# The first projections of an attention stage, issued in the tail of the stage before it

## The reference

```
h = rmsnorm(x, norm_pre) * (1 + scale) + shift
z = h @ w_in                       # 1024 x 3488, split into 14 parts
o_mla  = mha(q from rmsnorm(m_cq) @ wq_b, k and v from rmsnorm(m_ckv) @ wkv_b)   # 4 heads of 64+32
o_gqa  = gqa(rope(rmsnorm(g_q)), rope(rmsnorm(g_k)), g_v)                        # 4 heads, 2 KV heads
o_diff = softmax(q0 k0) v - lam * softmax(q1 k1) v, rmsnorm over each head       # 4 heads, 2 maps
o_hy   = hyena(hy_in)              # a long convolution of order 2, as DFT matmuls
out = concat(o_g * silu(gate_g) for the four groups) @ w_out
x = x + gate * rmsnorm(out, norm_post)
```

## Time and profile before

| | |
|---|---|
| median of three runs | 2651.21 us |
| the profiled execution, device time | 2656.59 us |
| its span, first to last instruction | 2654.8 us |
| TensorE matmul busy | 2388.5 us, 90% |
| VectorE, ScalarE, GpSimd busy | 1318.4 (50%), 909.7 (34%), 172.8 us (7%) |
| mean granted TensorE clock | 0.961 of 2.4 GHz |
| DMA | 129.11 MB, mean 49 GB/s |

### The profile page before, as it was taken

How to read it: one execution, slowest core, us unless ns; L and a number is a source line. 1 busy time by engine, 2 the same in 40 slices (tenths; PEclk the granted TensorE clock), 3 DMA queues, 4 the chain that set the end, 5 groups by cost and what they waited for, 6 DMA issues and landing times. The chain is left out here.

```text
span 2654.8 us, 36377 instructions
## 1 busy us (share of the span) xinstructions
PE 2388.5 (90%) x14472; PEld 1601.8 (60%) x14472; DVE 1318.4 (50%) x2642; ACT 909.7 (34%) x1826; POOL 172.8 (7%) x183
## 2 busy tenths in 40 slices
PE   3999999898999897989949999998989998889898
PEld 1755775675466766764417657656844666767643
DVE  3352663564556466581133526645644563855711
ACT  1142213452245264371022421134521452644610
POOL 0220001000100000001202200010001000000012
PEclk8999999999999998999959999999999999989999
DMA  6440000100100000012145301001000000001111
GB/s 223 152 162 26 21 31 17 49 2 14 34 32 1 10 3 6 33 34 87 63 156 178 136 26 52 10 7 49 1 14 34 33 1 12 1 6 65 41 64 56
DMA packets 74225, 129.11 MB, mean 49 GB/s; under 512 B 24994, under 2 KB 38178, under 8 KB 72420
## 3 DMA queue, kind: packets, MB, share of 16 engines
q1 hardware_dynamic: 73944, 122.04, 13.4%
q10 hardware_dynamic: 112, 4.72, 0.5%
HBM read 109.54 MB, written 21.92 MB: 50 GB/s over the span
## 5 line engine op out<-in xcount | busy, mean ns | idle before, releaser
L602 PE MATMUL psum<-arena 128*32 128x128 f32 (+8 forms) x9904 | 1727.8, 404 | 114.7 <-DMA arena<-in_hy_decay 47.4
L602 PEld LDWEIGHTS psum<-arena 128*128 128x128 f32 (+3 forms) x9904 | 1044.4, 155 | 735.0 <-issue 515.0
L606 PE MATMUL psum<-ident,arena 128*128 128x128 f32 (+1 forms) x2248 | 354.2, 282 | 92.6 <-ACT arena L1408 39.8
L1581 DVE TENSOR_TENSOR arena<-arena 128x64 f32<-128x64 f32 (+10 forms) x670 | 301.8, 497 | 199.3 <-ACT arena L1537 57.7
L606 PEld LDWEIGHTS psum<-ident,arena 128*128 128x128 f32 (+1 forms) x2248 | 254.5, 141 | 195.5 <-issue 106.0
L602 PE MATMUL psum<-k_parts,q_parts 96*128 96x384 f32 (+2 forms) x1000 | 285.1, 374 | 17.1 <-ACT arena L1332 4.7
L1581 DVE TENSOR_TENSOR arena<-psum,arena 128x512 f32<-128x512 f32 (+2 forms) x116 | 67.1, 580 | 280.4 <-PE psum L602 280.0
L1873 DVE TENSOR_REDUCE st<-psum 128x1 f32<-128x1152 f32 (+1 forms) x144 | 177.9, 1237 | 49.6 <-PE psum L602 49.2
L602 PEld LDWEIGHTS psum<-k_parts,q_parts 96*128 96x128 f32 (+1 forms) x1000 | 171.0, 195 | 34.4 <-issue 18.0
L1951 DVE TENSOR_REDUCE st<-psum 128x1 f32<-128x1152 f32 (+1 forms) x144 | 173.2, 1233 | 36.1 <-PE psum L602 35.9
L1332 ACT ACTIVATE arena<-psum,st 128x1152 f32<-128x1152 f32 (+1 forms) x144 | 162.4, 1128 | 75.6 <-DVE st L1873 72.5
(11 more groups left out here) (132 smaller groups left out, 1324.0 us busy)
## 6 DMA issues: line engine op xcount, KB each, us to landing
arena<-in_ada_w SPq DMA_DIRECT2D x12, 2048.0 KB, 8.8
arena<-in_w_in SPq DMA_DIRECT2D x10, 2048.0 KB, 9.1
arena<-out_xs SPq DMA_DIRECT2D x36, 512.0 KB, 4.8
out_xs<-arena SPq DMA_DIRECT2D x18, 512.0 KB, 2.6
arena<-in_w_out SPq DMA_DIRECT2D x4, 2048.0 KB, 8.5
out_xs<-in_x ACTq DMA_DIRECT2D x1, 4608.0 KB, 17.8
spectrum_kept<-arena SPq DMA_DIRECT2D x2, 2304.0 KB, 8.4
arena<-spectrum_kept SPq DMA_DIRECT2D x2, 2304.0 KB, 8.5
```

Of the source, the lines that this page charges most:

```text
L602: return nc.tensor.matmul(out, lhsT, rhs, start=start, stop=stop)
L606: return nc.tensor.transpose(out, src, ident[0:n, 0:n])
L1581: return nc.vector.tensor_tensor(out, a, b, op)
```

## The change

Four things move.

1. TensorE issues the first projections of the coming stage in the tail of the stage before it: one of mla before the last turns of hyena (into bank 7), two of gqa in the mla tail, three of diff0 in the gqa tail, three of diff1 in the diff0 tail (into banks 0, 1, 2). At the tail's first such step TensorE first waits for the last two exponentials.
2. In the preparation of gqa, diff0 and diff1 one gate piece of 512 tokens comes ahead of the loop, and a second one ahead of the turn of tile 8. In a pass TensorE turns tile i-1 first and then projects tile i+1 (gqa) or i+2 (diff). In diff0 `prompt_values` fills the pass after the last projection. ScalarE and VectorE take the first gate piece with tile 0, the rest at the end as before. In mla projection 1 comes before `mla_latent(0)`.
3. The parameters are loaded earlier, into parts of `arena` that are free by then: mla's after the last inverse transform is in PSUM, gqa's after the last scores of mla, diff0's behind the diff weights in the gqa attention, the rope table and cached keys of diff1 behind turns in diff0's tail. The cached values keep their wait for the stage, under the names `gqa_values` and `diff_values`, for which TensorE now waits before attention.
4. `K.restart` sets the turn of the banks so that they follow on the projections made ahead.

No instruction is added but waits; every projection and gate piece is made once, with the same shape.

The diff, cut to its core (of the offsets at the top only some are shown, and VectorE's lines follow ScalarE's):

```diff
-ROPE_GQA = ROPE_DIFF = SPLIT + 2 * 896
-CKEY = ROPE_GQA + NT * 128
+ROPE_GQA = OT + 4 * TOK
+GAINS = ROPE_GQA + NT * 128
+ROPE_DIFF = (DQ + 128, SPLIT + 2 * 896)
+CKEY_DIFF = SPLIT + 2 * 896 + NT * 128
...
+AHEAD = {"mla": 1, "gqa": 2, "diff0": 3, "diff1": 3}
...
+    def restart(self, b):
+        self.turn = b - 1
...
@@ sync @@
-                sp.wait_ge(*stage_value(2))
+                sp.wait_ge(*K.full(("Yp", 1)))
                 load(at(ROPE_MLA, NT, 64), I["rope"][:, :, 0:64], "mla_params")
...
-                sp.wait_ge(*stage_value(3))
+                sp.wait_ge(*S.at("scores", ("mla", len(UNITS["mla"]) - 1)))
                 load(at(ROPE_GQA, NT, 128), I["rope"][:, :, 64:192], "gqa_params")
...
+                sp.wait_ge(*stage_value(3))
+                load(at(VV + CACHE * GW, P), I["cache_gqa_v"][0][bass.ds(l, 1)].rearrange("o p h n -> (o p) (h n)"), "gqa_values")
...
-                sp.wait_ge(*stage_value(4))
+                load(at(ROPE_DIFF[0], NT, 64), I["rope"][:, :, 0:64], "diff_rope", 0)
...
                 for part in range(2):
                     if part == 1:
-                        sp.wait_ge(*stage_value(5))
-                    load(at(ROPE_DIFF, NT, 64), I["rope"][:, :, 0:64], "diff_rope", part)
+                        sp.wait_ge(*S.at("turned", ("diff0", piece_number("diff0", 14, 2))))
+                        load(at(ROPE_DIFF[1], NT, 64), I["rope"][:, :, 0:64], "diff_rope", 1)
+                        sp.wait_ge(*S.at("turned", ("diff0", piece_number("diff0", 15, 2))))
...
@@ tensor: end of hyena @@
+                weights("mla")
+                project("mla", "proj", 0, "mla", 0, 416, [7])
                 for t in range(TT):
-                    out_tile("hy", t, zv[:, t, 2, :], K.next())
+                    out_tile("hy", t, zv[:, t, 2, :], K.front())
+                K.restart(0)
                 stage_end(pe)
@@ tensor: diff_project, new @@
+                def diff_project(grp, i, banks):
+                    ps = claim(("proj", grp, i), banks)
+                    for k in range(KD):
+                        w = W[:, SLOT["diff", 0], k, :].rearrange("p (a b n) -> p a b n", a=2, b=2)
+                        last = mm(ps[:, 0:256], hT[:, k, i * P:(i + 1) * P], w[:, :, int(grp[4]), :],
+                                  k == 0, k == KD - 1)
+                    last.then_inc(*K.done(("proj", grp, i)))
@@ tensor: end of a step of attention(grp) @@
+                        if g == len(units):
+                            pe.wait_ge(*S.at("exps", (grp, g - 2)))
+                            pe.wait_ge(*S.at("exps", (grp, g - 1)))
+                        if grp == "mla" and g in (len(units), len(units) + 2):
+                            weights("gqa")
+                            project("gqa", "proj", (g - len(units)) // 2, "gqa", 0, 512, [(g - len(units)) // 2])
+                        if grp == "gqa" and len(units) <= g < len(units) + 3:
+                            weights("diff")
+                            diff_project("diff0", g - len(units), [g - len(units)])
@@ tensor: end of a step of diff_attention(grp) @@
+                        if grp == "diff0" and g == len(units):
+                            pe.wait_ge(*S.at("exps", (grp, 2 * g - 2)))
+                            pe.wait_ge(*S.at("exps", (grp, 2 * g - 1)))
+                        if grp == "diff0" and len(units) <= g < len(units) + 3:
+                            diff_project("diff1", g - len(units), [g - len(units)])
@@ tensor: mla preparation @@
                 for i in range(TT + 3):
+                    if i == 0:
+                        project("mla", "proj", 1, "mla", 0, 416, K.next())
                     if 1 <= i <= TT + 1:
                         mla_latent(i - 1)
-                    if i < TT:
-                        project("mla", "proj", i, "mla", 0, 416)
+                    if 1 < i < TT:
+                        project("mla", "proj", i, "mla", 0, 416, K.next())
@@ tensor: gqa, diff0, diff1 preparation @@
-                    for i in range(TT + 1):
-                        if i < TT and grp == "gqa":
-                            project(grp, "proj", i, grp, 0, 512)
-                        elif i < TT:
...
-                        if i >= 1:
-                            parts_turned(grp, i - 1)
+                    gate(grp[:4], vg, vg0, f, 0, K.next())
+                    for i in range(1, TT + 1):
+                        if i == TT:
+                            gate(grp[:4], vg, vg0, f, 1, K.next())
+                        parts_turned(grp, i - 1)
+                        t = i + AHEAD[grp] - 1
+                        if t < TT and grp == "gqa":
+                            project(grp, "proj", t, grp, 0, 512, K.next())
+                        elif t < TT:
+                            diff_project(grp, t, K.next())
+                        elif t == TT and grp == "diff0":
+                            prompt_values()
+                    gate(grp[:4], vg, vg0, f, 2, K.next())
                     if grp == "gqa":
-                        for f in range(2):
-                            for i in range(3):
-                                gate("gqa", "gqa_gate", 0, f, i, K.next())
...
+                        for i in range(3):
+                            gate("gqa", "gqa_gate", 0, 1, i, K.next())
                     parts_turned(grp, TT)
                     if grp != "diff1":
-                        pe.wait_ge(*S.at(f"{chunk_name}_params"))
+                        pe.wait_ge(*S.at(f"{grp[:4]}_values"))
@@ scalar: gqa, diff0, diff1 preparation @@
+                    order = six if grp == "gqa" else [(int(grp[4]), i) for i in range(3)]
                     for i in range(TT + 1):
...
+                        if i == 0:
+                            gate_tanh(grp[:4], *order[0], order)
                         if i >= 1:
                             parts_turned(i - 1)
...
+                    for f, i in order[1:]:
+                        gate_tanh(grp[:4], f, i, order)
                     parts_turned(TT)
```

More of the change, by code:

```diff
@@ L1099, in _ @@
                 pe.wait_ge(*K.emptied(("kT", TT)))
+                K.restart(AHEAD["gqa"])
                 attention("mla")
@@ L1153, in _ @@
                     pe.wait_ge(*K.emptied(("kT", grp, TT)))
+                    K.restart(AHEAD["diff0"])
                     if grp == "gqa":
@@ L2099, in _ @@
                         v.wait_ge(*S.at("diff_rope", int(grp[4])))
+                    order = six if grp == "gqa" else [(int(grp[4]), i) for i in range(3)]
+                    og = OT + (2 if grp == "gqa" else 4) * TOK
                     if grp == "diff0":
@@ L2127, in _ @@
                             nc.vector.memset(st[:, 72:73], 0.0).then_inc(*S.up("state_ready", grp))
-                    if grp == "gqa":
-                        for f, i in six:
-                            gate_finish("gqa", f, i, six, OT + 2 * TOK)
-                    else:
-                        f = int(grp[4])
-                        for i in range(3):
-                            gate_finish("diff", f, i, [(f, i) for i in range(3)], OT + 4 * TOK)
+                        if i == 0:
+                            gate_finish(grp[:4], *order[0], order, og)
+                    for f, i in order[1:]:
+                        gate_finish(grp[:4], f, i, order, og)
                     if grp == "diff0":
```

50 lines of the change are left out of this document (15 added, 35 removed).

## The result

The changed kernel takes 2592.43 us, the median of four runs (2588.53 to 2592.48), beside 2651.3 for the kernel before in the same group of runs (2651.1 to 2653.65). The medians lie 58.9 us apart, a quotient of 0.9778; the ratio on record for this group is 0.9762 [0.9742, 0.9782], which would be 63 us, and the quotient lies inside its interval. The forecast was 2588 (63 less), in a range of 2577 to 2608. Two later groups gave 65.8 us (2655.69 to 2589.91) and 66.8 us (2657.99 to 2591.21), so the kernel before varied more between groups than the changed one.

What follows compares the result with a forecast made beforehand. TensorE, busy 90% of the span, was taken as the bound, losing time to waits and low clock at stage boundaries. Boundary gains of 69 us less 6 for low clock gave 63, so some 2588 us, range 2577 to 2608.

Steps and rivals of the forecast that it cites:

- The boundaries: Four stage changes per layer, hyena to mla through diff0 to diff1: closing TensorE's holes gains 69 us over both layers.
- The 0.3 us for a meeting: At a stage change, a meeting of the engines right behind a matmul was taken to cost TensorE 0.3 us.
- the first head sum with its turn: In diff0's tail: head sums 1.9 us and a turn 0.2; the last head sum with root and product 2.7, uncovered.
- tile 0's chain in diff0: At diff0's start: the chain should end under the 6.9 us gate piece, between 0 and 1.6 us late, taken as 0.
- The margin of 0.4 us at gqa's second turn: In gqa's preparation: tile 1 is ready at 15.5 us, needed at 15.9; failure costs a microsecond or two per preparation.
- The loads' cover: Early parameter loads on SyncE: gqa's have 6 us to spare; without cover gqa would pay 3 to 10 us a layer.
- The price of the rival: Late load or copy at stage starts: 10 us a layer in gqa, 2 in each diff half, 28 in all.
- The allowance for low clock: Low-clock stretches of 1 to 2.5 us at four of eight boundaries: 6 us off the gain, bounds 0 and 20.
- From the profiled time to the median: Whole run: 63 us taken off both the profiled 2656.6 (2593.6) and the median 2651.2 (some 2588).
- Low clock comes back: Rival, at boundaries: slow stretches only move into projections or gate pieces behind holes; 20 us lost, 2602; chance 0.13.
- A late load: Rival, at stages' first tiles: late parameters or a delayed copy hold them; 28 us lost, 2610; chance 0.09.
- The work moves and nothing comes back: Rival, tails and preparations: tails grow 64 us in all, preparations don't shrink; 64 slower, 2715; chance 0.04.

Runs made afterwards that it cites:

- experiment 3: The changed kernel with the four parameter loads waiting for their stages again, as in the kernel before: 2629.95 us, ratio 0.9901 to the kernel before.
- experiment 8: The changed kernel unaltered, timed again in the second group: 2589.91 us, ratio 0.9746 to the kernel before.
- experiment 10: The changed kernel unaltered, timed once more in the third group: 2591.21 us, ratio 0.9755 to the kernel before.
- experiment 2: The changed kernel with all gate pieces of gqa and diff back behind the loop, tail projections and early loads kept: 2644.94 us, ratio 0.9955.
- experiment 5: The kernel before with only the early parameter loads and their new places in `arena`, TensorE's order unchanged: 2645.06 us, ratio 0.9959.
- experiment 1: The changed kernel with its tail projections put back behind the meeting of the stages, ahead of the first gate piece: 2615.78 us, ratio 0.9848.
- experiment 4: The changed kernel with the second gate piece put back behind the turn of tile 8, only the first ahead: 2605.38 us, ratio 0.9812.

## Why the prediction was right, by its own steps

**The boundaries, forecast 69 us together.** From the same instructions as in the earlier trace rows: mla to gqa took 107.6 us in both layers (forecast 107.5), gqa to diff0 62.1 (61.9), diff0 to diff1 63.7 (63.7), hyena to mla 18.7 in both (18.4; the 1.08 of the row at 414.38 against the 1.0 assumed, and a wait of some 0.2 for bank 7, which had been put at 0.3 at most). The gains are 4.7 twice, 12.7 and 12.0, 10.8 and 8.4, 7.3 twice: 67.9 us. Each boundary holds to 0.3 us: the first turn of gqa stands 8.1 us behind the meeting, the passes take 7.8 to 7.9, no wait on a split exceeds 1 us. The 0.3 us for a meeting, for which no row of before stood, is 0.26 where TensorE comes last. Not every piece was right, though the sums don't show it. In diff0's tail the first head sum with its turn takes 2.7 us (1015.26 to 1017.95), where I had 1.9 and left out the wait for ScalarE that stood there before too; the last one takes 2.1 (1025.55 to 1027.63), where I had 2.7. That they nearly cancel is luck. And tile 0's chain in diff0, which I put between 0 and 1.6 us longer than the gate piece, is far shorter: VectorE starts at 871.56 and has the split at 875.00, 3.7 us before the turn, which comes when the gate piece is through (878.68):

```profile
874.72 0.28 DVE L1610 TENSOR_TENSOR split_buf<-arena,split_buf 128x128 fp32r<-128x128 f32 x1
```

The 8.5 us that I read off were mostly the wait for the loads. By these rows a shorter piece might do in diff0; no run tried it.

**The margin of 0.4 us at gqa's second turn** held, barely: VectorE finishes tile 1's split at 660.28 and the turn starts at 660.56 without a wait, behind this copy:

```profile
651.82 0.60 ACT L1309 ACTIVATE arena<-psum 128x512 f32<-128x512 f32 x1 [5.37 <-PE psum L612]
652.32 0.47 ACT L1568 COPY arena<-psum 128x384 f32<-128x384 f32 x1
```

**The loads' cover** of 6 us held: ScalarE and VectorE wait for none of them. The price of the rival was put too low. I had 28 us in all, 10 a layer in gqa and 2 in each diff half; experiment 3 has 37. The 10 of gqa was right (10.5 and 11.2); missed were diff0, 5.1 and 6.2 us, and mla, some 4 us a layer, which I had not priced, while diff1 lost nothing.

**The allowance for low clock, 6 us at four boundaries, is the term that was mis-sized.** At the boundaries it is nothing: clock 1.00 in all. But 3.8 us (67.9 − 64.1) were lost between the boundaries, which I had priced at no change. With both layers together, mla from its projection 2 to its tail is 2.9 us longer, gqa's attention 3.2, diff0's attention 3.7 shorter, and all the rest 1.4 longer. From mla's projection 2 to its first scores it takes 79.2 us against 77.8 (79.1 in layer 1): the holes at the end, 2.18, 1.85 and 0.74 us, are as before, but the piece between the first two runs slow now. TensorE there, before:

```profile
489.59 2.40 PE L602 MATMUL psum<-arena 128*128 128x384 f32 x6
```

and after:

```profile
485.30 4.10 PE L612 MATMUL psum<-arena 128*128 128x384 f32 x6
```

In layer 0 gqa's attention took 123.4 us against 121.7, and diff0's 88.5 against 90.4. The stretches of after, gqa's attention and 30 us near its end:

```profile
735.60:859.00 123.40, 115.81 (x1130) 83.13 (x1131) 77.41 (x125) 63.28 (x106) 0.00 (x0) 0.99 0.07 21
830.00:860.00 30.00, 26.47 (x270) 18.53 (x268) 14.96 (x31) 12.72 (x27) 0.00 (x0) 0.94 0.00 1
```

In experiment 8 that attention took 121.8 us, at clock 1.00. Over whole profiles the loss is 3.8 us in the result's, 1.2 in experiment 8's and 2.2 in experiment 10's (spans of 2588.1 and 2589.1, with the same boundaries), against one profile of before. So the sum came out right (64.1 against 63) with the allowance in the wrong place, and partly by luck: nothing in the working says why 1 to 4 us should be lost there.

**From the profiled time to the median.** I subtracted 63 from the median. The profiled execution of before was 5.3 us over its median and the one after 0.1: 64.1 − 5.3 + 0.1 = 58.9, the gain measured. Most of the 4.4 us by which the forecast is low is this: the gain was read off an execution 5.3 us slower than the median one. Whether low clock made it slower isn't shown, since no clock of those others is on record. The two other groups, with 65.8 and 66.8, lie on the other side of 63.

**The rivals.** *Low clock comes back*, 2602: not so at the boundaries, and 1 to 4 us of it between them. The Trainium skill ("TensorE: Matmul & The Clock Gate", "A second HAM failure mode: psum-queue depth-cycling") reports a kernel whose clock swings because it goes round the PSUM banks each iteration with small idle times between its groups of matmuls. This trace doesn't agree: gqa's loop still goes round the banks, and it and the boundaries have 1.00. *A late load*: no. *The work moves and nothing comes back*, which I gave 0.04, comes half true when the gate pieces don't lie ahead: experiment 2, at 0.9955, gains nothing over experiment 5, at 0.9959, which has no projection in a tail; but it is not 64 us slower than the kernel before either. In this change the pieces keep it from coming true. (In that rival 634.70 to 647.1 is 12.4 us and not 12.7; the sum of 32 a layer stands.)

**What each part is worth**, by ratios to the changed kernel's 0.9762 of 2651: the tails 23 us, the gate pieces ahead 51 (13 of them the second), the early loads 37. They add to 111 where the change gave 59, since each is worth this only beside the others. Put the other way, early loads and gate pieces without tails (experiment 1) keep all but these 23. The new order within a pass, mla's projection 1 ahead and the turn of the banks were in all of these runs; of them only the second has a price, the 4.7 us a layer at hyena to mla, and that holds with the loads early: late, they cost 4 of it (experiment 3), and early by themselves they left the holes of 3.40 and 1.02 us as they were:

```profile
410.62 0.90 PE L611 MATMUL psum<-ident,arena 128*128 128x128 f32 x3 [3.40 <-DVE arena L2035]
```

Where the changed kernel lost a cover of the chain, the waits for a split tell most of the time: 2.4 us in the changed kernel, then 12.9 more in experiment 4, 24.9 more in 3, 44.3 more in 2, of spans that are 12.6, 41.4 and 52.5 us longer. All idle time of TensorE together is 12.8, 31.4 and 41.4 us more there, and its busy time 0.2 less, 10.0 and 11.1 more. In experiment 1 it is 13.1 and 10.2, of 23.3, and none of that is a split (1.8 us); these are the waits for copies and squares.

## What to carry to other kernels

Work issued ahead of a meeting fills holes in the tail, but doesn't start the chain behind the meeting sooner while another engine's first step waits for it; so keep independent work of the chain's length (here a gate piece of 6.9 us over a chain of 8 in gqa; in diff0 it is 3.4, and the piece is longer than it need be) for the place right behind the meeting, and have the chain's parameters there by then. Price a hole together with the slow instructions behind it: 1.0 to 1.8 us for each microsecond of idle time in experiments 1 to 4. Before a gain read off one profiled execution is taken from a median, see how far that execution lies from its own median.

## What was not expected of the hardware

- With the boundaries closed, the places between them, which the change does not touch, did not keep their time: in layer 1 gqa's attention is 1.4 us longer and diff0's 1.7 shorter, the same in three profiles. In layer 0 the granted clock differs between executions of one kernel (0.62 and 1.00 at mla's first scores), and the whole time by up to 8 us within a group (2582.83 to 2590.82).
- A meeting costs TensorE 0.26 us when it comes last and 0.96 to 1.47 when another engine still drains (rows at 407.12, 644.68 and 1027.63).
- A kernel whose order is 3 us shorter measured 6.0 and 9.4 us faster; 4 to 5 us of that are clock, at places where the order is the same.
